# A transformer layer with 32 experts on one core: four matrices' transfers issued in another place, smaller pieces at the ring's first refills and at its end, a shorter last pair

## What is computed

```python
xn = rmsnorm(x, g_mix)
q, k, v, u_pool, q_mem, gate_logits = split(xn @ w_in)
y_attn = (rmsnorm(diff_attention(q, k, v, lam)) * (1 - LAMBDA_INIT)) @ w_b_attn
y_pool = multiscale_pool(u_pool) @ w_b_pool
y_mem  = memory_cross_attention(q_mem, mem) @ w_b_mem
g = sigmoid(gate_logits + b_gates)                    # three gates of 1024 columns
h = x + (g[0] * y_attn + g[1] * y_pool + g[2] * y_mem) @ w_out
t = rmsnorm(h, g_ffn)                                 # 256 tokens x 1024
gates = softmax of the 4 largest of t @ w_router + b_router, of 32 experts
for e in 32 experts, for the tokens that chose e:
    g = min(t @ w_gate[e] + b_gate[e], 7);  u = clip(t @ w_up[e] + b_up[e], -7, 7)
    out += weight * ((g * sigmoid(1.702 * g) * (u + 1)) @ w_down[e] + b_down[e])
return h + out
```

## Time and profile before

| | |
|---|---|
| median of 3 runs (lowest to highest) | 1214.23 us (1214.15 to 1214.35) |
| the profiled execution's own time | 1214.63 us |
| its span in the profile | 1212.8 us |
| TensorE busy, mean granted clock | 1169.5 us (96%), 0.990 |
| VectorE, ScalarE, GpSimd busy | 436.5, 260.5, 43.7 us |
| moved by DMA | 460.67 MB (decimal), 380 GB/s over the span |

### The profile page before, as it was taken

The page is one execution under the profiler, slowest core; times in us unless marked ns, Lnnn a source line. Parts: engine busy times, 40 slices in busy tenths (PEclk is TensorE's granted clock), DMA queues, the critical chain, the costliest instruction groups (busy, mean ns, idle before and its releaser), DMA issues.

```text
span 1212.8 us, 13717 instructions
## 1 busy us (share of the span) xinstructions
PE 1169.5 (96%) x5436; PEld 581.0 (48%) x5436; DVE 436.5 (36%) x758; ACT 260.5 (21%) x463; POOL 43.7 (4%) x72
## 2 busy tenths in 40 slices
PE   9999999999999999999999999989898989899998
PEld 5888888888434344342434343433333343433342
DVE  5788798665222222222222121212122222221222
ACT  5655477542110110111010001101010101010101
POOL 1321101100000000000000000000000000000000
PEclk9999999999999999999999999999999999999999
DMA  9745645689999999999999999999999999999995
GB/s 384 267 148 185 214 142 186 224 363 394 406 427 431 427 432 432 431 432 431 430 431 430 429 429 432 431 432 431 431 431 432 432 432 431 431 431 431 425 428 232
DMA packets 28172, 460.67 MB, mean 380 GB/s; under 512 B 3216, under 2 KB 3984, under 8 KB 6608
## 3 DMA queue, kind: packets, MB, share of 16 engines
q1 hardware_dynamic: 27008, 456.34, 89.4%
q0 software_dynamic: 960, 3.41, 0.9%
q10 hardware_dynamic: 144, 0.03, 0.0%
HBM read 458.72 MB, written 1.05 MB: 379 GB/s over the span
## 4 chain that ended last, share of the span: by engine, by line
PE 66%; DMA 32%; issue 1%; DVE 1%; POOL 0%; SPq 0%; DVEq 0%; POOLq 0%
DMA experts_ring<-in_w_up 32%; PE bank L1773 25%; PE bank L1483 19%; PE bank L1818 7%; PE bank L1701 5%; PE bank L1761 2%; PE bank L1783 2%; PE bank L1447 1%; PE bank L1476 1%; PE bank L1784 1%; DMA raw<-in_mixer_halves 0%; PE bank L1847 0%; PE bank L1693 0%; PE bank L1602 0%; PE bank L1798 0%
## 5 line engine op out<-in xcount | busy, mean ns | idle before, releaser
L1773 PE MATMUL bank<-experts_ring,region 128*64 128x512 f32 x2048 | 468.4, 608 | 31.9 <-DMA experts_ring<-in_w_gate 21.2
L1773 PEld LDWEIGHTS bank<-experts_ring,region 128*64 128x64 f32 x2048 | 150.2, 139 | 325.5 <-issue 317.5
L1818 PE MATMUL bank<-experts_ring,region 128*64 128x512 f32 x1024 | 228.7, 596 | 2.1 <-DMA experts_ring<-in_w_down 1.9
L1483 PE MATMUL bank<-hi_split,region_split 128*128 128x512 f32 x400 | 151.3, 401 | 0.0
L1818 PEld LDWEIGHTS bank<-experts_ring,region 128*64 128x64 f32 x1024 | 73.6, 137 | 137.6 <-issue 136.4
L1483 PE MATMUL bank<-raw_split,region_split 128*128 128x512 f32 x336 | 130.9, 389 | 0.0
L944 ACT ACTIVATE region<-region 128x512 f32<-128x512 f32 x32 | 20.1, 629 | 452.3 <-DVE region L1409 452.3
L973 DVE TENSOR_TENSOR raw_split<-raw,hi_split 128x2048 fp32r<-128x2048 f32 x42 | 96.1, 2288 | 33.9 <-ACT hi_split L693 33.7
L1417 DVE TENSOR_SCALAR region<-bank 128x512 f32<-128x512 f32 x32 | 22.1, 692 | 236.7 <-PE bank L1784 236.7
L1409 DVE TENSOR_SCALAR region<-bank 128x512 f32<-128x512 f32 x32 | 22.1, 691 | 226.3 <-PE bank L1784 226.3
L1483 PEld LDWEIGHTS bank<-hi_split,region_split 128*128 128x128 f32 x400 | 75.1, 188 | 17.4 <-issue 2.6
(11 more groups left out here) (183 smaller groups left out, 760.2 us busy)
## 6 DMA issues: line engine op xcount, KB each, us to landing
experts_ring<-in_w_gate SPq DMA_DIRECT2D x26, 4096.0 KB, 36.6
experts_ring<-in_w_up SPq DMA_DIRECT2D x26, 4096.0 KB, 38.8
experts_ring<-in_w_down SPq DMA_DIRECT2D x26, 4096.0 KB, 39.2
raw<-in_mixer_halves SPq DMA_DIRECT2D x44, 1024.0 KB, 5.0
experts_ring<-in_w_up SPq DMA_DIRECT2D x10, 2048.0 KB, 11.1
experts_ring<-in_w_down SPq DMA_DIRECT2D x9, 2048.0 KB, 14.2
experts_ring<-in_w_gate SPq DMA_DIRECT2D x8, 2048.0 KB, 23.3
experts_ring<-in_w_gate SPq DMA_DIRECT2D x8, 1024.0 KB, 9.3
```

The lines of the kernel that those rows point to most:

```text
L1483: ins = nc.tensor.matmul(unit_bank(u)[:, :], a[:, k, toks], b[:, cols], start=(k == 0 and m == 0), stop=(k == k_n - 1 and m == 2))
L1773: ins = nc.tensor.matmul(dst[h * SLOTS:(h + 1) * SLOTS, :], XE[:, kk, e * SLOTS:(e + 1) * SLOTS], w[:, k, h * HALF:(h + 1) * HALF], start= ...
L1818: ins = nc.tensor.matmul(bank[(2, 1)[e]][h * SLOTS:(h + 1) * SLOTS, :], AHT[e][:, k, half * SLOTS:(half + 1) * SLOTS], w[:, k, h * HALF:(h ...
```

## The change

Eight things are done.

1. Buffers: `region1` and `region7` change places in the memory that the ring shares; gate "a", the merged branches and the low parts of two operands move to regions 4, 6 and 3; the biases of the experts go into `con`. So places 4 and 9 of the ring are free earlier.
2. SP now issues half-matrix 4 after mixer half 34, half-matrix 9 after mixer half 36, the bias of gate "a" just ahead of it (it was POOL's), half-matrix 0 after mixer half 37, half-matrix 2 after mixer half 40. Half-matrix 1 is now two of 1 MB: the first follows mixer half 38. Its second goes to `SPARE` (region 6, outside the ring), issued after the last unit. In the ring the place of that second quarter is filled at once with the second quarter of half-matrix 11.
3. The first refill, half-matrix 10, comes as 0.5, 0.5 and 1 MB; the last half-matrix as 1, 0.5 and 0.5 MB, each with its wait in TensorE.
4. `w_router` and `b_down` (still POOL's) are loaded later; `combine` waits for them.
5. The last pair leaves out the dispatch for a pair that does not follow (TensorE), its slots and weights (VectorE) and its copies (ScalarE).
6. TensorE's first five pairs are written out ahead of the loop; ScalarE and VectorE loop over three pairs.
7. The four last products and stores go by column half first, and each waits for its half alone.
8. VectorE: both `add_bias` of units 36 and 37 after the split of mixer half 36; the router weights' gain after `add_h(45)`.

```diff
-        buffers = ("region9", "mem_low", "x_low", "region7", "hi4", "raw4", "region2", "region8", "hi0", "raw0",
-                   "hi1", "raw1", "hi2", "raw2", "hi3", "raw3", "region1", "region10",
+        buffers = ("region9", "mem_low", "x_low", "region1", "hi4", "raw4", "region2", "region8", "hi0", "raw0",
+                   "hi1", "raw1", "hi2", "raw2", "hi3", "raw3", "region7", "region10",
...
+            def refill_part(i, part, landing):
+                n, h = divmod(RING + i, 2)
+                sp.dma_start(ring_half(RING + i)[:, part], expert_rows(...)[:, h * 4096 + part.start:h * 4096 + part.stop]
+                             ).then_inc(landing, 16)
...
-                for i in range(2):
-                    part = slice(i * 2048, (i + 1) * 2048)
+                for i, part in enumerate((slice(0, 2048), slice(2048, 3072), slice(3072, 4096))):
                     sp.dma_start(ring_half(PER_ROUND - 1)[:, part], rest[:, part]).then_inc(last_in[PER_PAIR - 1 + i], 16)
 
             for H in range(HALVES + 1, 2 * N0):
+                load(H)
+                if H == 2 * PIECES.index("ga1"):
+                    sp.wait_ge(qk_done, HEADS)
+                    load_half(0, 4)
+                if H == 2 * PIECES.index("wba0"):
+                    sp.wait_ge(pv_done, HEADS)
+                    for t in range(NT):
+                        sp.dma_start(G["a"][:, t, :], b_gates[0:D].rearrange("(a n) -> a n", a=1).to_broadcast([P, D])
+                                     ).then_inc(gbias_in[2], 16)
+                    sp.wait_ge(merged, 4)
+                    load_half(0, 9)
+                    biases()
                 if H == 2 * PIECES.index("wba0") + 1:
-                    sp.wait_ge(pv_done, HEADS)
-                    biases()
-                    sp.wait_ge(merged, 4)
                     load_half(0, 0)
-                load(H)
-                if H == 2 * PIECES.index("wba1") + 1:
+                if H == 2 * PIECES.index("wba1"):
                     sp.wait_ge(oT_done, HEADS)
-                    load_half(0, 1)
-                if H == 2 * PIECES.index("wo0") + 1:
+                    sp.dma_start(ring_half(1)[:, 0:2048], expert_rows(0, 0)[:, 4096:6144]).then_inc(second_in[0], 16)
+                    refill_part(1, slice(2048, 4096), quarter_in[1])
+                if H == 2 * PIECES.index("wo0"):
                     sp.wait_ge(unit_done, UNIT_OF[("ga1", NT - 1, 0)] + 1)
                     load_half(0, 2)
             sp.wait_ge(unit_done, UNIT_OF[("wba1", NT - 1, 0)] + 1)
             load_half(0, 3)
-            sp.wait_ge(mgT_done, 4)
-            load_half(0, 4)
...
             half_free(sp, 2 * PIECES.index("wo1") + 1)
+            sp.dma_start(SPARE, expert_rows(0, 0)[:, 6144:8192]).then_inc(spare_in, 16)
             load_half(0, 8)
-            load_half(0, 9)
...
+            for k in range(2):
+                sp.wait_ge(quarter_used, k + 1)
+                refill_part(0, slice(k * 1024, (k + 1) * 1024), quarter_in[0])
+            sp.wait_ge(used, 1)
+            refill_part(0, slice(2048, 4096), piece_in[0])
+            sp.wait_ge(quarter_used, 3)
+            refill_part(1, slice(0, 2048), second_in[0])
...
             def combine(it, tile):
+                pe.wait_ge(late_in, 32)
...
-                pe.wait_ge(hn_ready, NT)
-                dispatch(it + 1)
+                if more:
+                    pe.wait_ge(hn_ready, NT)
+                    dispatch(it + 1)
...
-                            if g == PER_ROUND - 1 and k == 2:
-                                pe.wait_ge(last_in[PER_PAIR], r * 16 + 16)
+                            if g == PER_ROUND - 1 and k >= 2:
+                                pe.wait_ge(last_in[PER_PAIR + k - 2], r * 16 + 16)
...
-            with pe.Fori(0, TURNS) as d:
+            for s in range(TURN_PAIRS):
+                pair_products(0, 0, s, spare=(s == 0))
+            with pe.Fori(1, TURNS) as d:
                 for s in range(TURN_PAIRS):
                     pair_products(0, d, s)
...
-            pair_products(0, 0, PAIRS - 1)
+            pair_products(0, 0, PAIRS - 1, more=False)
...
-            pe.wait_ge(o_lo, last * 2 + 2)
-            pe.wait_ge(o_hi, last * 2 + 2)
             pe.wait_ge(wT_copied, last + 1)
-            for j in range(4):
-                t, h = divmod(j, 2)
+            for h in range(2):
+                pe.wait_ge((o_lo, o_hi)[h], last * 2 + 2)
```

More of the change, by code:

```diff
@@ L345, in decoder_layer @@
         second_in = {i: sem(f"second_in{i}") for i in range(0, RING, 2)}
-        last_in = [sem(f"last_in{i}") for i in range(PER_PAIR + 1)]
+        last_in = [sem(f"last_in{i}") for i in range(PER_PAIR + 2)]
         gbias_in = [sem(f"gbias_in{i}") for i in range(3)]
@@ new lines, in pair_copies @@
+            def pair_copies(it, more):
+                for e in range(2):
+                    act.wait_ge(g_read, it * 2 + (e + 1))
+                    nc.scalar.activation(SG, GS, ACT.Sigmoid, scale=ALPHA).then_inc(sig_done, 1)
+                for e in range(2):
+                    act.wait_ge(actT_done, it * 2 + (e + 1))
+                    nc.scalar.activation(AHT[e], bank[(2, 0)[e]][:, :].rearrange("p (j s) -> p j s", j=4),
+                                         ACT.Copy).then_inc(actT_copied, 1)
+                    if e == 0:
+                        act.wait_ge(slots_free, it + 1)
+                        act.wait_ge(comb_done, it * 4 + 4)
+                        nc.scalar.activation(PWT, bank[3][:, 0:SEQ], ACT.Copy).then_inc(wT_copied, 1)
+                        if more:
+                            xe_lower_half(it + 1, it * PER_PAIR + 8)
+                for e in range(2):
+                    act.wait_ge(used, it * PER_PAIR + (10 + 2 * e))
+                    nc.scalar.activation(OE[e * SLOTS:(e + 1) * SLOTS, 0:HALF], bank[(2, 1)[e]][0:SLOTS, :],
+                                         ACT.Copy).then_inc(o_lo, 1)
@@ L960, in _, with round_copies @@
+            def round_copies(first):
+                with act.Fori(0, (PAIRS - 1) // 3) as d:
+                    for s in range(3):
+                        pair_copies(first + d * 3 + s, True)
+                pair_copies(first + (PAIRS - 1), False)
+            round_copies(0)
+            with act.If(n_rounds > 1):
+                with act.Fori(1, n_rounds) as r:
+                    xe_lower_half(r * PAIRS, r * PER_ROUND)
+                    round_copies(r * PAIRS)
         @block.vector
@@ L1240, in _ @@
                     head_weights(h + 1)
-                unit(22 + 2 * h)
+                if h + 1 < HEADS:
+                    unit(22 + 2 * h)
+                else:
+                    lo_after(36)
                 if h:
                     oT_lower(h - 1)
-            unit(37)
+            lo_after(37)
+            add_bias(36)
+            add_bias(37)
             oT_lower(HEADS - 1)
@@ new lines, in round_results @@
+            def round_results(first):
+                with dve.Fori(0, (PAIRS - 1) // 3) as d:
+                    for s in range(3):
+                        pair_results(first + d * 3 + s, d * 3 + s, True)
+                pair_results(first + (PAIRS - 1), PAIRS - 1, False)
+            round_results(0)
+            with dve.If(n_rounds > 1):
+                with dve.Fori(1, n_rounds) as r:
+                    nc.vector.tensor_scalar(RANK, RANK, -float(SLOTS), None, ALU.add).then_inc(rank_ready, 1)
+                    dve.wait_ge(rank_ready, r)
+                    dve.wait_ge(slots_free, r * PAIRS)
+                    for t in range(NT):
+                        expert_slots(0, t)
+                    expert_weights(0)
+                    xe_upper_half(r * PAIRS)
+                    round_results(r * PAIRS)
@@ L1442, in _ @@
+            add_results(n_rounds * (4 * PAIRS), range(4), (6, 7, 0, 2), by_half=True)
         @block.tensor
@@ L1762, in combine, with project @@
                                      start=True, stop=True).then_inc(comb_done, 1)
-            def project(it, r, d, s, e, m, first, dst, between=None):
+            def project(it, r, d, s, e, m, first, dst, between=None, spare=False):
                 for j in (first, first + 1):
```

222 lines of the change are left out of this document (96 added, 126 removed).

## The result

| | before | the change |
|---|---|---|
| median (lowest to highest) | 1214.19 us (1214.01 to 1214.35), 4 runs | 1221.89 us (1221.04 to 1225.26), 4 runs |
| ratio, 95% interval | | 1.0069 (1.0049 to 1.0088) |
| profiled execution, its span | 1214.63, 1212.8 | 1225.26, 1223.5 |
| experts' start (first product of pair 0) | 302.39 | 311.14 |

The change is slower by 7.7 us. The prediction said 1216.9, at most 1219.0, so the time lies outside its range. It put slower (0.37) behind no change (0.44); the direction was not foreseen clearly.

A forecast was written before the change was run, and what follows sets the result against it. The prediction took TensorE to bound two thirds of the kernel and the experts' weight transfers one third. Profiled 1214.63, wait +3.0, clock +1.7, lead -1.9, end -0.1 gave 1217.3, as a median 1216.9 us; range 1210.8 to 1219.0.

The forecast's parts named there:

- the wait: At unit 42's 13th product TensorE waits for mixer half 39 and its splits: 3.0 us slower, between 1.5 and 4.2.
- the lead: In the experts' weight stream, a fuller ring gains 1.9 us (0.9 to 2.9), capped by the transfer issued at 344.74.
- so I add 1.6, not 2.7: In SP's queue, mixer half 39 lands 1.6 us after the byte count's 256.0; the check on half 38 was 2.7 late.
- Mixer half 37 (lands about 243, wanted by 243.6) and half 38 (about 250, by 251.8) come just in time by the same count.: In SP's queue ahead of half 39, both halves land before TensorE wants them, so they add no wait.
- The clock: Behind TensorE's gap at unit 42 the granted clock falls for some 4 us: 1.7 us slower, counted as likely.
- The end: In the last pair, half-matrix 190 lands at 1196.8 and 7.1 us of products follow: gain 0.1 us, at best 1.0.
- the first turn: TensorE's first five pairs written out save a 2.54 us jump at 568.57; a later weight wait makes it worth nothing.
- the last pair's dispatch: Leaving out 32 products (3.6 us) of TensorE in the last pair gains nothing, since the stream lands where it landed.
- the pieces: Finer first refills gain nothing of their own, extra 0.5 MB transfers cost nothing, and halving the last MB buys nothing.
- the worst, 1219.1: Rival: the wait at its upper end, 4.2 us, with the clock and a lead of only 0.9; 1219.1 us, chance 0.08.
- Experts starting at 305 to 307: Sign that the forecast holds: in the profile after, the experts start at 305 to 307 us instead of 302.4.
- a stream whose early transfers still take 9 us: Sign that the forecast is wrong: early expert weight transfers still take 9 us, where some 7.2 was expected.

The follow-up runs named there:

- the second trace: The unaltered change measured and traced once more, against the kernel before: 1222.21 us against 1214.72, ratio 1.0059.
- only9: The change with half-matrix 9 issued behind half-matrix 3 instead of ahead of mixer half 37: 1215.24 us, ratio 1.0004 to the kernel before.
- bias_on_pool: The change with the last gate's bias issued by POOL on its own queue instead of by SP: 1220.35 us, ratio 1.0049 to the kernel before.
- swap37: The change with mixer half 37 issued ahead of half-matrix 9 and the expert biases: 1223.20 us, ratio 1.0071 to the kernel before.
- full_ring: order_fixed with half-matrix 4 issued early and half-matrix 9 right behind half-matrix 3: 1214.46 us, ratio 1.0000 to the kernel before.
- order_fixed: queue_as_before with mixer halves 37 and 38 issued ahead of half-matrix 0 and the expert biases: 1214.77 us, ratio 1.0002 to the kernel before.
- rolled: order_fixed with TensorE's first five pairs put back into the loop of turns: 1214.97 us, ratio 1.0002 to the kernel before.
- full_ring_coarse: The change with five transfers reordered in SP's queue and half-matrix 10 refilled as two of 1 MB: 1215.03 us, ratio 1.0003 to the kernel before.
- queue_as_before: The change with the weights' order of before and no spare quarter, gate bias still on SP: 1215.74 us, ratio 1.0011 to the kernel before.
- behind39: The change with half-matrix 0 and the quarters of half-matrices 1 and 11 issued behind mixer half 39: 1220.81 us, ratio 1.0050 to the kernel before.

## Why the prediction was wrong

**The mechanism of the loss was right.** The mixer halves are late behind the weights in SP's one queue, TensorE waits at unit 42's 13th product, the clock falls behind the gap, and nothing absorbs it up to the experts. Two terms of the sum were wrong in size: the wait, and the lead, whose cap was put in the wrong place.

**The step that failed first: "so I add 1.6, not 2.7: half 39 lands at 257.6, between 256.0 and 258.7".** It landed at 261.3 (260.6 in the second trace), 5.3 and 4.6 us behind the count of bytes. The count had been checked on a transfer of before and had come out 2.7 us short; I explained part of that away with two reasons that no row supported. only9 shows the offset without half-matrix 9 ahead: 8.25 MB behind 228.66 would be 251.1, and it was 254.7, 3.6 late. The gate bias is part of it. Before, on POOL's queue, the median of the six transfers of 512 KB was 4.6 us to landing, near the 4.7 of 1 MB of weights alone, and the trace of before had that row; I charged the bias by its bytes, "2.25 + 2.45", 233.4, and it landed at 236.2, 6.9 us after the issue of its second half. It is not all of it: without a gate bias in SP's queue the same count is still short, 2.7 before and 2.2 for half 37 in bias_on_pool. With half-matrix 9 in the queue too another 1 to 2 us beyond its bytes go; why is open. So the wait was 6.5 us against TensorE's own free run (6.3 in the second trace), not 3.0, and outside my 1.5 to 4.2.

**"Mixer half 37 (lands about 243, wanted by 243.6) and half 38 (about 250, by 251.8) come just in time by the same count."** Half 37 landed at 246.4 and gave the first gap; half 38 landed at 253.8. swap37 shows that being late with half 37 cost nothing of its own.

**The step that failed second: "I take 1.9 us" of lead, 0.9 to 2.9.** The runs show none: full_ring against order_fixed is 0.3 us, with intervals of 0.1% (1.1 us) on either. Under 1 us of lead could hide in that, 1.9 hardly. I had looked for the tightest point among the later refills, start + 42 and + 92 us, and found 1.95 us. The tight stretch is earlier, in the first 40 us, where the refills wait for TensorE one by one and a full ring makes the DMA engines pause. The transfer that was to land after some 7.2 us took 10.3 in the change (9.7 in the second trace), and 8.7 and 8.2 where no half is late (full_ring, only9).

**The clock:** forecast 1.7, and the 45.5 us from 265.61 to the experts' start are 44.0 in only9 (43.6 before): 1.6 lost. Right.

**The end** (forecast 0.1), **the first turn, the last pair's dispatch, the pieces, `w_router`, `b_down`, `add_bias`** (counted at nothing): as a sum order_fixed bears it out. By themselves only the first turn (rolled) and the pieces of half-matrix 10 (full_ring_coarse) were tried; among the others a small gain could hide a small loss. The gate bias on SP was not free, though: in queue_as_before it brings a gap of 0.75 us and 0.9 us of time. I had looked at who waits for the bias itself (hidden, as said) and not enough at what stands behind it.

The sum with measured sizes, from the second trace: TensorE goes on at 264.91 instead of 258.8, 6.1 (forecast 3.0); from there to the start it takes 45.5 us instead of 43.6, 1.9, of which the clock is some 1.5 (forecast 1.7); the rest is 0.4 us shorter (forecast 2.0). That is 7.6 against a forecast of 2.7, and 7.7 and 7.5 between the medians of the two measurements. Of the 4.9 us that were missing 3.1 are the wait, 1.6 the lead and the end. Of the rivals none had it; the worst, 1219.1, was short by the same two terms. "Experts starting at 305 to 307" in "what would show it" was the test that failed, and "a stream whose early transfers still take 9 us" the one that came true.

## What to carry to other kernels

Where one queue serves two consumers, an early transfer is paid for by whatever stands behind it; moving it ahead was free here where the queue was idle, so look for the idle stretch first and count all later transfers with due times, not only the next one. When a count of bytes is short on a transfer that can be checked, keep the whole difference. And filling a buffer earlier gains only as much as the refills behind it can follow: here they wait for the consumer, and the gain went in the pauses.

## What the runs showed of the hardware

- DMA engines fully busy (1.01) moved 242 GB/s in the 5 us of the gate bias (order_fixed), and 414 in the next 5. That is some 2 us of queue more than the bytes of these two transfers, which read one 4 KB row for each of 128 partitions (an estimate, (414 - 242) x 5 / 414). Before, on POOL's queue, six such transfers of 512 KB, issued in pairs, landed after 3.9 to 4.2 us (the first of a pair) and 4.9 to 5.9 us (the second).
- The same transfer on a second queue beside a full one landed after 11.45 us; the first queue's next mixer half came 3.0 us sooner for it, and the same 4.25 MB were all in 2.5 to 2.7 us sooner (14.8 us against 17.3 and 17.5).
- Gaps of 2.37 us (behind39), 3.55 us (bias_on_pool) and 1.87 us (ahead of the change's last eight products) were followed by a granted clock of 0.66 in the next 5 us; one of 2.54 us in the change was not (1.00), nor one of 1.94 us at the same place before the last products in the kernel before. Length alone doesn't say whether it falls.
- The 16 parts of one transfer land apart by some 2 us at 350 us and by 8.2 at 1190 us before, by 2 to 3 and by 8.7 in the change, by 1.8 and 7.0 in full_ring. Why one part lags more and more, and whether it takes the last microsecond of lead with it, was not tried.
